# The source of a 128-fold copy of a bias row: a DRAM line instead of four SBUF partitions

## What is computed

```python
def _swiglu(xn, w_gate, w_up, w_down):
    return (jax.nn.silu(xn @ w_gate) * (xn @ w_up)) @ w_down

# in the attention, for each block of 128 queries and each of 4 heads
bucket = _t5_bucket(kpos[None, :] - qpos[:, None])
bias = jnp.take(rel_bias, bucket, axis=0).transpose(2, 0, 1)     # rel_bias: 32 buckets x 4 heads
logits = jnp.einsum('bhtqd,bhtkd->bhtqk', qblk, kt) + bias[None, :, None]

# first block, for each layer: a mixer (conv, pool, attention, conv), then the SwiGLU
x = x + _rms(m, g[1])
x = x + _rms(_swiglu(_rms(x, g[2]), w_gate, w_up, w_down), g[3])
```

## Time and profile before

| what | value |
|---|---|
| median of three runs | 2283.48 us (2283.34 to 2283.98) |
| span of the profiled execution | 2282.2 us |
| mean granted TensorE clock | 0.980 |
| PE busy with matmuls | 2183.5 us (96%) |
| DVE busy | 1277.5 us (56%) |
| ACT busy | 992.4 us (43%) |
| POOL busy | 118.0 us (5%) |
| DMA, mean over the span | 172 GB/s, 392.43 MB |

### The profile page before, as it was taken

The page is one execution under the profiler, slowest core; times in us unless marked ns, Lnnn a source line. Parts: engine busy times, 40 slices in busy tenths (PEclk is TensorE's granted clock), DMA queues, the critical chain, the costliest instruction groups (busy, mean ns, idle before and its releaser), DMA issues.

```text
span 2282.2 us, 35632 instructions
## 1 busy us (share of the span) xinstructions
PE 2183.5 (96%) x15124; PEld 2027.6 (89%) x15124; DVE 1277.5 (56%) x1340; ACT 992.4 (43%) x1074; POOL 118.0 (5%) x231
## 2 busy tenths in 40 slices
PE   7969988999989999999999999989999999998998
PEld 7869978998979998899989989879998998887998
DVE  5645455445565457645464556775455545777454
ACT  4433444434554344344343444654344334455433
POOL 0000011001010000100020010010002001001000
PEclk9989999999999999999999999999999999999999
DMA  7556546555446555555565553236556555424552
GB/s 253 185 142 213 187 158 183 185 184 185 148 134 199 184 185 183 177 176 185 185 215 186 185 184 125 88 122 199 184 184 217 185 184 166 130 75 157 185 184 92
DMA packets 288662, 392.43 MB, mean 172 GB/s; under 512 B 7512, under 2 KB 255112, under 8 KB 288416
## 3 DMA queue, kind: packets, MB, share of 16 engines
q1 hardware_dynamic: 280928, 368.21, 49.6%
q10 hardware_dynamic: 4032, 14.68, 2.0%
q0 software_dynamic: 3584, 7.84, 1.6%
HBM read 388.60 MB, written 2.10 MB: 171 GB/s over the span
## 4 chain that ended last, share of the span: by engine, by line
PE 88%; DVE 5%; DMA 2%; ACT 2%; POOL 2%; issue 1%; POOLq 0%; DVEq 0%; SPq 0%; ACTq 0%
PE psum L485 28%; PE psum L487 27%; PE psum L486 27%; DMA raw<-in_ffn_w_up 2%; ACT squares L982 1%; POOL mean L1764 1%; DVE w_lo L1284 1%; DVE Y L1725 1%; DVE xT_lo L1312 1%; POOL rstd L1769 1%; DVE Y L1304 1%; DVE X L1738 1%; PE psum L841 1%; PE psum L869 1%; PE psum L576 1%
## 5 line engine op out<-in xcount | busy, mean ns | idle before, releaser
L485 PE MATMUL psum<-xT_hi,w_hi 128*128 128x256 f32 x3264 | 931.8, 285 | 16.2 <-DVE w_lo L1284 14.9
L486 PE MATMUL psum<-xT_lo,w_hi 128*128 128x256 f32 x3264 | 926.1, 284 | 0.0
L487 PE MATMUL psum<-xT_hi,w_lo 128*128 128x256 f32 x3264 | 925.9, 284 | 0.0
L1284 DVE TENSOR_TENSOR w_lo<-raw,w_hi 128x2048 fp32r<-128x2048 f32 x349 | 784.9, 2288 | 206.4 <-ACT w_hi L954 205.8
L954 ACT ACTIVATE w_hi<-raw 128x2048 fp32r<-128x2048 f32 x349 | 656.9, 1907 | 76.2 <-PE psum L487 46.2
L485 PEld LDWEIGHTS psum<-xT_hi,w_hi 128*128 128x128 f32 x3264 | 623.9, 191 | 26.0 <-DVE w_lo L1284 15.1
L486 PEld LDWEIGHTS psum<-xT_lo,w_hi 128*128 128x128 f32 x3264 | 623.9, 191 | 4.4 <-issue 1.0
L487 PEld LDWEIGHTS psum<-xT_hi,w_lo 128*128 128x128 f32 x3264 | 623.9, 191 | 0.0
L1347 DVE TENSOR_TENSOR h_full<-gate,psum 128x512 f32<-128x512 f32 x80 | 55.1, 688 | 471.1 <-PE psum L487 471.1
L487 PE MATMUL psum<-w_hi,h_lo 128*128 128x512 f32 x768 | 302.0, 393 | 0.0
L485 PE MATMUL psum<-w_hi,h_hi 128*128 128x512 f32 x768 | 300.3, 391 | 0.0
(11 more groups left out here) (214 smaller groups left out, 1341.3 us busy)
## 6 DMA issues: line engine op xcount, KB each, us to landing
raw<-in_ffn_w_in SPq DMA_DIRECT2D x88, 1024.0 KB, 5.1
raw<-in_ffn_w_gate SPq DMA_DIRECT2D x44, 1024.0 KB, 5.3
raw<-in_ffn_w_up SPq DMA_DIRECT2D x44, 1024.0 KB, 5.3
raw<-in_ffn_w_down SPq DMA_DIRECT2D x44, 1024.0 KB, 4.9
raw<-in_ffn_w_out SPq DMA_DIRECT2D x44, 1024.0 KB, 4.9
raw<-in_mix_w_in SPq DMA_DIRECT2D x28, 1024.0 KB, 5.3
raw<-in_conv_w_in SPq DMA_DIRECT2D x24, 1024.0 KB, 5.2
raw<-in_attn_w_qkv SPq DMA_DIRECT2D x12, 1024.0 KB, 5.2
```

Source lines behind the costliest of these rows:

```text
L485: pe.matmul(dst, l_hi, r_hi, start=first, stop=False, skip_group_check=loose)
L486: pe.matmul(dst, l_hi, r_lo, start=False, stop=False, skip_group_check=loose)
L487: return pe.matmul(dst, l_lo, r_hi, start=False, stop=last, skip_group_check=loose)
L1284: dve.tensor_tensor(w_lo[u % LO_RING][:], raw[u % LO_RING][:], f32(w_hi[u % HI_RING][:]), ALU.subtract).then_inc(lo_ready, 1)
```

## The change

The bias row of four partitions is first stored to a new DRAM tensor `bias_line` of 4 by 512 float32, 8 KB. POOL waits for that store. The DMA that writes each row 128 times into `bias_scratch` then reads from `bias_line` instead of from `bias_row`. Its destination, its size and its queue are as they were.

```diff
     scratch = nc.dram_tensor("bias_scratch", [4, P, 2 * S + 1], F32, kind="Internal").ap()
+    bias_line = nc.dram_tensor("bias_line", [4, 2 * S], F32, kind="Internal").ap()
...
         bias_copied = sem("bias_copied")
+        line_stored = sem("line_stored")
         scratch_stored = sem("scratch_stored")
...
                         pool.wait_ge(bias_copied, seen.next(bias_copied))
+                        pool.dma_start(bias_line, bias_row[:]).then_inc(line_stored, 16)
+                        pool.wait_ge(line_stored, seen.next(line_stored, 16))
                         pool.dma_start(scratch[:, :, 0:2 * S],
-                                       bias_row[:].unsqueeze(1).broadcast_to([4, P, 2 * S])
+                                       bias_line.unsqueeze(1).broadcast_to([4, P, 2 * S])
                                        ).then_inc(scratch_stored, 16)
                         pool.wait_ge(scratch_stored, seen.next(scratch_stored, 16))
```

## The result

The changed kernel takes **2267.03 us** (median of four runs, 2266.15 to 2269.64) against 2283.73 us for the kernel before in the same comparison (2283.34 to 2284.18). The ratio is 0.9922 with a 95% interval of 0.9908 to 0.9936: 16.7 us less, clear of noise. Forecast were 2266.7 us. The profiled execution took 2267.53 us, its span is 2265.7 us and its mean granted clock 0.984.

The account below looks back on a forecast made before the run. Matmuls on PE were taken to bound the kernel, except for a weight block held up by the bias copy. The profiled 2282.2 less 16.8 is 2265.4, plus 1.3 for the runs' median 2266.7 us; range 2262.5 to 2284.

Parts of the forecast that it names:

- What bounds the kernel, and where the 2% of DMA lie: Matmuls bound it, PE 88% of the chain; the DMA 2% is a stage 1 weight block delayed by the bias copy.
- What the stall costs, 16.76 us: Stage 1 takes 169.85 us by its `h_full` markers, stage 3 without the copy 153.09: surplus 16.76 us.
- The line's store: Storing `bias_row` to `bias_line` and POOL's wait: 2.9 us, ends 2.6 and 5.1, costing nothing on the path.
- The copy's rate: Copy from DRAM on four engines at 20 GB/s each: 13.1 us for the data, landing at 142.8.
- the upper side: Highest rate considered for the copy: 22 GB/s an engine, from the 1170 to 1172 us window with `cell_gain`.
- The deadline, 150.7: Latest copy landing without a PE stall: PE's restart less 14.85 us idle, less 5.64 us from landing to restart.
- The cap belongs to the source: The old copy's 27 GB/s come from its four SBUF source partitions, not from the destination.
- `windows` and `pool_scale` cost nothing in their new place: Stage 2 loads moving from 165.9 to about 143: 5 us of data an engine against 7.9 us of slack.
- Rival 1: Part of the stall stays, copy at 8 to 12.5 GB/s or loads colliding: 1 to 12 us, 2268 to 2279; chance 0.08.
- Rival 2: Cap belongs to destination rows or POOL's queue, so the change doesn't lift it: 2286.4 us, or 2288.6; chance 0.09.
- Rival 3: Rereading the same short DRAM row is slow, 4.8 GB/s an engine: stall 33.6 us, time 2302.2 us; chance 0.06.
- What would show it: Line lands in 2.6 to 5.1 us, POOL waits 15 to 25, copy alone 50 to 90 GB/s, PE's 14.85 us gone.

Follow-up runs that it names:

- every dose above: n of 128 copies made from SBUF in the old place, the others from `bias_line` a stage later: 2268.34 (80), 2273.69 (96), 2277.32 (112), 2283.73 us (128, before).
- the dose of 80: 80 of 128 copies made from SBUF in the old place, the others from `bias_line` a stage later: 2268.34 us, PE idle 2.50 us.
- 80, 96 and 112 copies: That many of 128 copies made from SBUF as before, the others from `bias_line` a stage later: 2268.34, 2273.69 and 2277.32 us.
- the new partitions: Kernel before, still copying from SBUF, with bias rows in partitions 0, 4, 8, 12 (2266.96 us) or 0, 32, 64, 96 (2266.24 us).
- the round pitch: Kernel before with `bias_scratch` rows of pitch 512 instead of 513: 2284.89 us, ratio 1.0001.
- the copy with 16 engines: Changed kernel with the copy's two outer dimensions exchanged, so 16 engines take part: 2265.47 us, with more runs 2269.94 us.

## Why the prediction was right

Point by point, as it was put.

- *What bounds the kernel, and where the 2% of DMA lie*: right. The stall of the earlier trace rows was tied to the copy in every dose above, and the block's wait for its share on four engines is seen between 152 and 158 us.
- *What the stall costs, 16.76 us*: right to the hundredth by the markers; 16.5 us of span, 16.7 us of median. That the median came within 0.4 us of the forecast is in part luck: the executions above differ by up to 2 us at the first marker alone. To lay stage 1 beside stage 3 was worth more than to add up the stall and the slow matmuls (16.5 us).
- *The line's store*: 2.0 us against 2.9, below the end of 2.6; together with the copy's issue it put the copy back by 2.26 us.
- *The copy's rate*: four engines again, as taken. Its time was mis-sized: 20.4 us to landing instead of 5.4 + 13.1 = 18.5. By the copy's packets (0.20 us for 4 KB) the 20 GB/s hold while an engine works on it; what was too small is the 5.4 for start, interleaved blocks and landing, which came to 7.3 here. It landed at 144.28, not 142.8, and cost nothing, since either is well ahead of the deadline. The reading behind the upper side was weak: `cell_gain` is the last of a row of tables in POOL's queue, and the window from 1170 to 1172 us doesn't tell which of them moved. The DRAM to DRAM figure of the Trainium skill's "DMA: Bandwidth & Descriptors", section "Latency and other measured facts", 12.9 an engine as an estimate, was too low for these four engines while they worked.
- *The deadline, 150.7*: too late by 1.9 us. The constant behind it (5.64 us from landing to restart) was read at one landing and doesn't carry to others: 4.29 of it are fixed, the rest of the block isn't. With the measured rate that changed nothing; at the 12.9 GB/s of that estimate, a landing at 150.0, it would have: 1.2 us of stall, where the prediction said the same time in the end. That is small, and no run had just that rate; the dose of 80 shows the kind of loss.
- *The cap belongs to the source*: right, and now shown rather than argued, by moving the source only.
- *`windows` and `pool_scale` cost nothing in their new place*: right; they are issued at 144.56, and no wait of PE lies behind them. They did use slack: DVE's wait before the marker at 162.59 is 2.86 us, and 7.12 before the same marker of the kernel without the copy.
- *Rival 1* (part of the stall stays) didn't come about here, but is just what 80, 96 and 112 copies show. *Rival 2* is refuted by the new partitions and the round pitch. *Rival 3* shows only in the copy with 16 engines, mildly (13 GB/s each, 7 in the window above), and there a quarter of the data an engine hides it.
- *What would show it*: the wait of POOL, 19.51 us, is inside 15 to 25; the 14.85 us are gone; the copy's 66 GB/s are inside 50 to 90, at 20.6% of the engines. The line's 2.0 us are below the 2.6 to 5.1. A share where the copy runs alone couldn't be read: other loads were in flight all along.

## What to carry to other kernels

A transfer that nobody waits for can stop the kernel by what it does to the DMA engines it shares: when a weight block lands late, look for the slow transfer in flight with it, and read from share and GB/s how many engines it holds and at what rate. A DMA whose engines all reread partitions 0 to 3 of SBUF crawled at 27 GB/s; with the rows four partitions apart, or by way of a small line in DRAM, an engine's rate was three times as high, with rows 32 apart twice. To price such a stall, lay the stage beside a twin that has the same code without the transfer.

## What the runs showed of the hardware that I had not expected

- Four engines that read SBUF partitions 0 to 3 get 27 GB/s together, partitions 0, 32, 64 and 96 some 59 while they work on the copy, partitions 0, 4, 8 and 12 some 78 and rows from DRAM some 81 (0.60, 0.28, 0.21 and 0.20 us for a packet of 4 KB). SBUF at its best and DRAM are alike here, though the landings of 17.3 and 20.4 us suggest otherwise.
- Packets of two queues took turns on an engine, though their sizes differ: the late block moved one packet of 1 KB (0.045 us) for each of 4 KB from the slow copy (0.62 us), 36 beside 37 in 6 us.
- What the clock takes for an idle stretch did not grow with it in these traces. Idle times of 2.50, 5.62, 11.21 and 14.85 us, and 15.45 in the kernel with rows of round pitch, were followed by 0, 27, 16, 18 and 28 matmuls at the lower level. With 5.62 us the clock was still 0.99 from 158 to 160, while PE stood still, and 0.50 from 160 on, just as the work came back: a stall of two fifths of the length lost more to the clock.
- The same kernel on 16 copying engines was granted 0.84 or 0.95 of the clock in the same stretch of 32.5 us, in two executions on two chips, and its medians were 4.5 us apart.
